# Two squared-ReLU MLPs of a two-block decoder kernel: first product with the weights held still, and no transposes

## What is computed

```python
def squared_relu_mlp(x, w1, w2):            # x: 256 x 1024, w1: 1024 x 4096, w2: 4096 x 1024
    return jnp.square(jax.nn.relu(x @ w1)) @ w2

for i in range(2):
    x = layer_norm(ALPHA * x + mix, ...)
    ff = squared_relu_mlp(x, mlp_w1[i], mlp_w2[i])
    pe = jax.nn.sigmoid(x @ ple_gate_w[i] + ple_gate_b[i]) * (p[i] @ ple_proj[i])
    x = layer_norm(ALPHA * x + ff + pe, ...)
...
h = h + moe(rmsnorm(h, ln2), w_router, ..., w_up, b_up, w_down, b_down)     # 32 experts
h = h + (p_2 @ w_ple) * jax.nn.sigmoid(rmsnorm(h, ln_ple) @ w_ple_gate)      # the last gate
return rmsnorm(h, ln_f)
```

## Time and profile before

| | before |
|---|---|
| median of 3 runs | 2122.85 us (2118.32 to 2123.15) |
| the profiled execution | 2115.99 us, span 2114.3 us |
| PE busy | 1989.3 us, 94% |
| VectorE (DVE), ScalarE (ACT) busy | 701.0 us (33%), 432.0 us (20%) |
| HBM read | 541.37 MB, 257 GB/s over the span |
| granted TensorE clock, mean | 0.966 of 2.4 GHz |
| from 0 to 70 us | pooling mixer, norm, first gate |
| 70 to 263 us, 586 to 778 us | the two MLPs |
| 263 to 586 us, 778 to 1042 us | delta rule; attention and router |
| 1042 to 2066 us | the experts |
| 2066 to 2114 us | last gate, norm, store |

### The profile page before, as it was taken

How to read it: one execution, slowest core, us unless ns; L and a number is a source line. 1 busy time by engine, 2 the same in 40 slices (tenths; PEclk the granted TensorE clock), 3 DMA queues, 4 the chain that set the end, 5 groups by cost and what they waited for, 6 DMA issues and landing times.

```text
span 2114.3 us, 22692 instructions
## 1 busy us (share of the span) xinstructions
PE 1989.3 (94%) x8850; PEld 1199.4 (57%) x8850; DVE 701.0 (33%) x986; ACT 432.0 (20%) x667; POOL 13.7 (1%) x21
## 2 busy tenths in 40 slices
PE   6999999989999999987899999999999999999997
PEld 4688787687478879664544444434444344444333
DVE  3555533474355550252212222122121322222122
ACT  0444422112144431043101101101010001101003
POOL 0000000000000000000000000000000000000000
PEclk9999999999999999868899999999999999999999
DMA  9354522200454461204388999999998999999972
GB/s 381 134 210 173 203 96 80 80 0 35 165 209 159 192 264 51 80 1 167 135 319 367 409 377 421 389 395 409 375 422 363 422 408 376 408 376 422 388 317 100
DMA packets 67809, 543.36 MB, mean 257 GB/s; under 512 B 7552, under 2 KB 7552, under 8 KB 10528
## 3 DMA queue, kind: packets, MB, share of 16 engines
q1 hardware_dynamic: 65296, 533.53, 61.9%
q0 software_dynamic: 2160, 7.87, 1.1%
q10 hardware_dynamic: 288, 1.05, 0.1%
HBM read 541.37 MB, written 1.05 MB: 257 GB/s over the span
## 4 chain that ended last, share of the span: by engine, by line
PE 90%; DVE 5%; ACT 2%; DMA 1%; issue 1%; POOL 0%; DVEq 0%; SPq 0%; ACTq 0%; POOLq 0%
PE ps L1998 16%; PE ps L1984 10%; PE ps L2013 8%; PE ps L613 6%; PE ps L615 6%; PE ps L614 6%; PE ps L503 5%; PE ps L2027 5%; PE ps L936 3%; PE ps L1145 3%; PE ps L2089 2%; PE ps L1345 2%; PE ps L2076 1%; PE ps L944 1%; PE ps L2058 1%; PE ps L1350 1%
## 5 line engine op out<-in xcount | busy, mean ns | idle before, releaser
L1998 PE MATMUL ps<-ring,arena 128*64 128x512 f32 x1536 | 334.9, 594 | 0.0
L1998 PEld LDWEIGHTS ps<-ring,arena 128*64 128x64 f32 x1536 | 108.2, 137 | 214.3 <-issue 214.3
L2223 DVE TENSOR_SCALAR arena<-ps 128x512 f32<-128x512 f32 x40 | 27.7, 691 | 598.7 <-PE ps L1998 344.6
L1984 PE MATMUL ps<-ring,arena 128*128 128x512 f32 x512 | 222.3, 592 | 0.0
L613 PE MATMUL ps<-ring_split,arena_split 128*128 128x512 f32 x512 | 205.6, 402 | 7.5 <-DVE ring_split L769 7.5
L615 PE MATMUL ps<-ring_split,arena_split 128*128 128x512 f32 x512 | 203.8, 398 | 0.0
L614 PE MATMUL ps<-ring_split,arena_split 128*128 128x512 f32 x512 | 203.5, 397 | 0.0
L769 DVE TENSOR_TENSOR ring_split<-ring,ring_split 128x1024 fp32r<-128x1024 f32 x128 | 155.4, 1223 | 121.0 <-ACT ring_split L821 121.0
L2013 PE MATMUL ps<-ring,arena 128*64 128x512 f32 x768 | 170.1, 595 | 0.0
L1984 PEld LDWEIGHTS ps<-ring,arena 128*128 128x128 f32 x512 | 97.2, 190 | 116.1 <-issue 114.8
L821 ACT CAST ring_split<-ring 128x1024 fp32r<-128x1024 f32 x128 | 132.9, 1049 | 111.5 <-PE ps L615 111.5
(11 more groups left out here) (368 smaller groups left out, 2035.6 us busy)
## 6 DMA issues: line engine op xcount, KB each, us to landing
ring<-experts_dram SPq DMA_DIRECT2D x384, 1024.0 KB, 10.5
ring<-weights_dram SPq DMA_DIRECT2D x57, 2048.0 KB, 8.8
row_buf<-rows_dram POOLq DMA_DIRECT2D x15, 512.0 KB, 9.2
ring<-weights_dram SPq DMA_DIRECT2D x3, 1024.0 KB, 11.4
tab<-tables_dram SPq DMA_DIRECT2D x1, 2285.0 KB, 17.6
x<-tokens_dram SPq DMA_DIRECT2D x1, 1024.0 KB, 5.0
arena<-rows_dram SPq DMA_DIRECT2D x2, 512.0 KB, 18.8
xT<-weights_dram SPq DMA_DIRECT2D x1, 1024.0 KB, 6.9
```

The lines of the kernel that those rows point to most:

```text
L1984: ins = T.matmul(bank(2 * half_ + m), xs_big[:, 2 * c + d, :], w[:, d, m * STEP:(m + 1) * STEP], start=False, stop=c == 3 and d == 1, skip ...
L1998: ins = T.matmul(bank(first_bank + m)[at:at + SMALL], xs_small[:, 2 * c + d, SMALL * (j - 1):SMALL * j], w[half_][:, d, m * STEP:(m + 1) * ...
```

## The change

1. **`up` holds the weights still.** A block of 128 hidden channels of the weights is now the stationary operand, and all 256 tokens are the moving one. The result has hidden channels on the partitions, as `down` wants them, so `turn` goes with its eight transposes. An `up` is 96 instructions of 256 columns (4 chunks, 2 rows of channels, 4 blocks, 3 products; L684 to L686 of the changed kernel) where it was 48 of 512. It writes `ps[:, 0]` in even steps and `ps[:, 1]` in odd ones.
2. **The hidden values.** One ReLU of 1024 columns (L754), then ScalarE squares twice: rounded into `hid_high` (L817) and in fp32 in place (L818); VectorE subtracts (L757). TensorE's order is the whole next `up`, then `down`. In ScalarE's and VectorE's order the splits of the next `up` come behind the hidden values.
3. **Step 0 is an exception to that**: there the splits for step 1's `up` come first, ahead of the ReLU and the squares. `first_up` is gone, and the last two steps lose their special order.
4. **The last gate's weights** are loaded once `moe_used` tells that all but the last 8 chunks of the experts are used; the wait stands behind the last expert load, and `moe_ring_done` is gone.

```diff
-            def up_tile(w, c, t):
-                for k in range(2):
-                    m = split_product(ps[:, 0, t * 512:t * 512 + 512], x_high[:, 2 * c + k, t * P:(t + 1) * P],
-                                      x_low[:, 2 * c + k, t * P:(t + 1) * P], w, k,
-                                      c == 0 and k == 0, c == 3 and k == 1)
-                return m
...
+            def up(s, par, first=False):
+
+                if first:
+                    pe.wait_ge(sem("ple_logit"), TILES * layer + par + 1)
+                else:
+                    pe.wait_ge(sem("mlp_relu"), 8 * layer + s - 1)
+                for c in range(4):
+                    high, low = weights_of(up_chunk(s, c) if not first or par else c, c)
+                    for k in range(2):
+                        for b in range(4):
+                            at = k * STEP + b * P
+                            out_ = ps[:, par, b * SEQ:(b + 1) * SEQ]
+                            xs = x_high[:, 2 * c + k, :], x_low[:, 2 * c + k, :]
+                            opens, last = c == 0 and k == 0 and b % 2 == 0, c == 3 and k == 1
+                            T.matmul(out_, high[:, at:at + P], xs[0], start=opens, stop=False, skip_group_check=True)
+                            T.matmul(out_, high[:, at:at + P], xs[1], start=False, stop=False, skip_group_check=True)
+                            m = T.matmul(out_, low[:, at:at + P], xs[0], start=False, stop=last, skip_group_check=True)
                     m.then_inc(sem("mlp_product"), 1)
-            def turn(s, par, first=False):
...
-                for t in range(TILES):
-                    for k in range(4):
-                        m = T.transpose(ps[:, 1, k * SEQ + t * P:k * SEQ + (t + 1) * P],
-                                        relu[:, par, t, k * P:(k + 1) * P], ident)
-                m.then_inc(sem("mlp_hid_psum"), 1)
...
             def step(s, par, first=False):
-                up(s + 1, (0,))
-                turn(s, par, first)
-                up(s + 1, (1, 2, 3))
+                up(s + 1, 1 - par, first)
                 down(s, par, first)
...
+            def step(s, par, first=False, last=False):
+                if first:
                     for c in range(4):
                         v_mlp_low(v, layer, up_chunk(s + 1, c), raw_up(1 - par, c), c)
-                v.wait_ge(sem("mlp_hid_high"), 8 * layer + s + 1)
-                V.tensor_tensor(hid_low[:, par], view(ps[:, 1, :], (4, SEQ)), hid_high[:, par], ALU.subtract)\
+                v.wait_ge(sem("mlp_product"), MLP_CHUNKS * layer + (4 if first else 8 * s))
+                V.tensor_scalar(squared[:, par], view(ps[:, par, :], (4, SEQ)), 0.0, None, ALU.max)\
+                 .then_inc(sem("mlp_relu"), 1)
+                v.wait_ge(sem("mlp_square"), 8 * layer + s + 1)
+                V.tensor_tensor(hid_low[:, par], squared[:, par], hid_high[:, par], ALU.subtract)\
                  .then_inc(sem("mlp_hid_low"), 1)
+                if not first and not last:
+                    for c in range(4):
+                        v_mlp_low(v, layer, up_chunk(s + 1, c), raw_up(1 - par, c), c)
...
+                if first:
+                    next_up()
+                a.wait_ge(sem("mlp_relu"), 8 * layer + s + 1)
                 if not early:
                     a.wait_ge(sem("mlp_product"), MLP_CHUNKS * layer + 8 * s - 4)
-                A.copy(hid_high[:, par], view(ps[:, 1, :], (4, SEQ))).then_inc(sem("mlp_hid_high"), 1)
+                A.activation(hid_high[:, par], squared[:, par], ACT.Square)
+                A.activation(squared[:, par], squared[:, par], ACT.Square).then_inc(sem("mlp_square"), 1)
+                if not first and not last:
+                    next_up()
...
+            sp.wait_ge(sem("moe_used"), PASS_CHUNKS * (n + 1) - 8)
...
-            fill(sp, "gate20", 0, "moe_ring_done", 1)
+            fill(sp, "gate20", 0)
             fill(sp, "gate21", 1)
```

More of the change, by code:

```diff
@@ L742, in step @@
             def step(s, par, first=False):
-                up(s + 1, (0,))
-                turn(s, par, first)
-                up(s + 1, (1, 2, 3))
+                up(s + 1, 1 - par, first)
                 down(s, par, first)
-            first_up()
+            up(0, 0, first=True)
             step(0, 0, first=True)
@@ L753, in pe_mlp @@
                 step(2 * i + 1, 1)
-            s = MLP_STEPS - 2
-            up(s + 1, (0,))
-            turn(s, 0)
-            up(s + 1, (1, 2, 3))
-            down(s, 0, chunks=(0, 1))
-            turn(s + 1, 1)
-            down(s, 0, chunks=(2, 3))
-            last_down(s + 1, 1)
+            step(MLP_STEPS - 2, 0)
+            last_down(MLP_STEPS - 1, 1)
             for slot in range(4):
@@ L778, in v_mlp @@
         def v_mlp(v, layer):
-            def step(s, par, first=False, early=False, last=False):
-                for t in range(TILES):
-                    if first and t == 0:
-                        v.wait_ge(sem("mlp_first"), layer + 1)
-                    elif first or t == 0:
-                        v.wait_ge(sem("mlp_product"), MLP_CHUNKS * layer + (4 if first else 8 * s))
-                        if not early:
-                            v.wait_ge(sem("mlp_hid_psum"), 8 * layer + s - 1)
-                    V.tensor_scalar(relu[:, par, t, :], ps[:, 0, t * 512:t * 512 + 512], 0.0, None, ALU.max)\
-                     .then_inc(sem("mlp_relu"), 1)
-                if not last:
+            def step(s, par, first=False, last=False):
+                if first:
                     for c in range(4):
                         v_mlp_low(v, layer, up_chunk(s + 1, c), raw_up(1 - par, c), c)
-                v.wait_ge(sem("mlp_hid_high"), 8 * layer + s + 1)
-                V.tensor_tensor(hid_low[:, par], view(ps[:, 1, :], (4, SEQ)), hid_high[:, par], ALU.subtract)\
+                v.wait_ge(sem("mlp_product"), MLP_CHUNKS * layer + (4 if first else 8 * s))
[3 more added lines that the diff above has]
+                V.tensor_tensor(hid_low[:, par], squared[:, par], hid_high[:, par], ALU.subtract)\
                  .then_inc(sem("mlp_hid_low"), 1)
+                if not first and not last:
+                    for c in range(4):
+                        v_mlp_low(v, layer, up_chunk(s + 1, c), raw_up(1 - par, c), c)
                 for c in range(4):
@@ L800, in v_mlp @@
              .then_inc(sem("mlp_side"), 1)
-            step(0, 0, first=True, early=True)
-            step(1, 1, early=True)
+            step(0, 0, first=True)
+            step(1, 1)
             with v.Fori(1, MLP_STEPS // 2 - 1) as i:
@@ L835, in a_mlp, with step, next_up @@
             base = mlp_base[layer]
-            def step(s, par, round_, early=False, last=False):
-                for t in range(TILES):
-                    a.wait_ge(sem("mlp_relu"), 16 * layer + 2 * s + t + 1)
-                    A.activation(relu[:, par, t, :], relu[:, par, t, :], ACT.Square).then_inc(sem("mlp_square"), 1)
-                if not last:
+            def step(s, par, round_, first=False, early=False, last=False):
+                def next_up():
                     slot = 2 * (1 - par)
@@ L854, in step @@
                     a_mlp_high(a, layer, down_chunk(s, c) - (4 if last else 0), raw_down(par, c), c)
-            step(0, 0, 0, early=True)
+            step(0, 0, 0, first=True, early=True)
             step(1, 1, 0, early=True)
```

26 lines of the change are left out of this document (1 added, 25 removed).

## The result

| | before | changed |
|---|---|---|
| median of 4 runs each | 2120.59 us | 2092.4 us |
| lowest, highest | 2117.87, 2123.15 | 2087.7, 2096.89 |
| ratio, 95% interval | | 0.9867 [0.9834, 0.99] |
| profiled execution, its span | 2115.99, 2114.3 | 2096.89, 2095.0 |

What follows compares the result with a forecast made beforehand. TensorE was taken to bound the two MLPs. The terms -13.9 - 11.0 + 0 - 0.5 sum to -25.4 us, taking 2122.85 to 2097.5 us, with a range of 2088 to 2116.

Steps and rivals of the forecast that it cites:

- Transposes, -13.9: MLP steps: removing 16 turns of eight transposes, 0.87 us each on TensorE's path, saves 13.9 us.
- p = 0.117, cost 0: MLP up: a 256-column product takes p = 0.117 us, half a 512-column one, so stationary weights cost 0.
- The choice of the rate: Split products in the MLPs: limited by how fast columns stream, not by an 18.7 ns charge per instruction.
- Rival 1: MLP up: a charge per product, p near 0.127 us, +16.4 us, total 2113.9 us; chance 0.18.
- rival 2: MLP up: loads and passes set the pace, p 0.1086 to 0.112, total 2085.2 to 2090.6 us; chance 0.08.
- rival 3: MLP up: weight load in series with its product, p = 0.221 us, +160 us, total 2258 us; chance 0.05.
- Splits ahead of the squares, -11.0: Second step of each MLP layer: earlier weight splits remove the 3.9 us stall and slow clock, 5.5 us a layer.
- Rival 4: Second MLP step: the stall stays because a later landing eats the 0.7 us of room; 2108.5 us, chance 0.07.
- The chain of ACT and DVE, 0: MLP steps: ReLU, squares, low part and next first split finish at 8.3 us, wanted at 11.2; margin 2.9, cost 0.
- The last gate, -0.5: Program end: gate weights loaded earlier, issued near 2020, remove the small wait before the ninth gate record; -0.5 us.
- The window: Each MLP layer's window: 192.17 us less 6.95 and 5.5, giving 179.7 us.

Runs made afterwards that it cites:

- down256: Changed kernel with each product of the down cut into two of 256 columns; 2094.97 us, ratio 0.9885.
- up128: Changed kernel with each product of the up cut into two of 128 columns, so 192 weight loads an up; 2259.53 us, one run.
- before_early: Kernel before, with only the second step's weight splits moved ahead of step 0's squares; 2121.8 us against 2118.99, ratio 1.0012.
- control: Changed kernel run once more, unaltered; 2089.78 us, ratio 0.9868.
- act_late3: Changed kernel with three needless 128x2048 copies on ScalarE ahead of each step's squares; 2158.16 us, one run.
- control_b: Changed kernel unaltered again, beside the two kernels with filler products for TensorE in the attention steps; 2095.45 us.
- gate_late: Changed kernel with the last gate's weights loaded behind the first product after the experts, as before; 2098.57 us, ratio 0.9903.
- late_splits: Changed kernel with step 0 in the order of other steps, ReLU and squares ahead of the second step's weight splits; 2112.93 us, ratio 0.9973.

## Why the prediction was right

- **Transposes, -13.9.** Right: eight transposes cost 0.874 us, 0.87 forecast, and all of it on PE's path.
- **p = 0.117, cost 0.** Right: 0.1167 in the timeline and 0.1170 over a layer ((179.37 - 384 x 0.2332)/768, the layer's opening included). The choice of the rate came from products of 512 columns at the lower level; `down256` and `up128` bear it out. Rival 1 is off by 10 ns, rival 2 by 5 to 8, rival 3 by 104. The figure of the Trainium skill ("TensorE: Matmul & The Clock Gate", Back-to-back issue gap), 109 ns for 256 columns, was rightly not followed: the trace has 117.
- **Splits ahead of the squares, -11.0.** The size is right for the change as a whole: 12.40 a layer measured, 6.95 + 5.5 forecast. The step's reason was incomplete. It argued that the splits held PE at 85.89, and left out that in the kernel before the second `up` also waits to overwrite the first one's banks. That wait went with the alternating banks of the new product, which the sum gives no part in this term. `before_early` gives +1.8 us for the same order where -11.0 would be due. Within the new product the order is worth 17.6 (8.8 a layer), since without it the stall there would be 6.0 us and the slow clock 2.8, and not 3.9 and 1.6.
- **Rival 4 was nearer than its 0.07.** The forecast had the first split ready at 81.3 and PE at 82.0, 0.7 us of room. It was ready at about 82.3 for 82.69 in the first layer, and 0.2 us late in the second: the load was issued at 71.7 and not 71.0 and took 8.3 us and not 8.0, in the second layer 8.9. The clock stayed at 1.00 behind the 0.2. That the room sufficed, here and with 0.9 and 0.2 us in `control`, is in part luck.
- **The chain of ACT and DVE, 0.** Right: 3.1 us of margin in the timeline and 2.9 by `act_late3`, 2.9 forecast, from durations of a kernel in which this chain didn't exist yet.
- **The last gate, -0.5.** Right in kind, small in size: 0.7 to 0.9. The loads were issued at 2029.51 and not near 2020. The last `up_small`, whose end they wait for, ends at 2024.3 here, and 5 more us pass before the issue; what SP does in them the trace doesn't show. It costs nothing, since the loads are issued 18 us ahead of the product that comes before the gate.
- **The window.** 179.7 forecast, 179.76 and 180.23 read; in `control` 179.37 by the other cut, which with the last product's 0.40 is 179.77.
- **The remaining 2.8 us** (28.2 for 25.4) are in nothing that was changed. `control` has -24.8 in the MLPs, -1.0 at the end, -1.0 in the experts, -2.5 in the attention stretch, and +2.8 and +0.8 in the delta rule and the start, together -25.7. The experts' stretch moves by itself: 1032.2 us in `before` and `control_b`, 1031.0 to 1031.3 in the other two profiles of the changed kernel, in `gate_late` and also in `before_early`, which has the old product and the old gate. And 2.8 us is less than a median of four runs moves: the three sets of runs of the changed kernel lie 28.2, 28.5 and 23.5 us below the kernel before that ran beside them. All 12 runs of the one have a median of 2093.0 us and all 39 of the other 2118.8, which is 25.8 us.
- **The starting point.** The forecast's 2097.5 us started from 2122.85, and the runs of the result put the kernel before at 2120.59. Of the 5.1 us between 2097.5 and 2092.4, 2.3 come from there.

## What to carry to other kernels

Halving an instruction's columns to make the other operand stationary is free as long as its stream (here 256 x 0.457 = 117 ns) stays over the least that a product with a load of its own takes (112 ns here); with 128 columns that floor, and no longer the columns, sets the time. Before moving an operand's preparation earlier, list everything that the consumer waits for, its output's banks above all: an order that is worth 8.8 us a layer with a free pair of banks is worth nothing without. Check when the first operand of a moved preparation is ready, too: here the room was between 0.9 us and 0.2 us too little. And measure a margin by spending it: one copy cost nothing, three gave a stall of the expected size.

## What the runs showed of the hardware

- Split (fp32r) products run at 0.456 ns a column at the granted clock 1.00 (0.417 would be one column a cycle at 2.4 GHz), and at just one a cycle at the lower level: 0.427 us for 512 columns. Against half of a plain fp32 record that is 9% more with 512 columns (233.2 for 214.5) and 8% with 256 (117.0 for 108.6), a rate and not a charge.
- The waits of 2.8 to 6.0 us on PE cost more than themselves: behind 6.0 us (`late_splits`) the granted clock was 0.50 for 4.6 us, 2.8 us more; behind 3.9 us it was 0.66, 1.6 us more; behind 2.8 us (`act_late3`) it fell as well. Behind 0.2 us it stayed at 1.00.
- The 12 runs of the changed kernel in these studies took 2087.7 to 2090.5 us (six) or 2095.4 to 2096.9 (six). Three of them were profiled, one of the cheaper kind and two of the dearer, and the difference is outside the MLPs: the delta rule's stretch (326.71 against 328.15 and 328.19) and the attention's (250.43 against 254.80 and 252.93), where the granted clock is 0.97 against 0.96 and 0.82 against 0.79 and 0.81. What decides between them was not found; added work for PE raised the clock and didn't shorten the time.
